# Two transformer blocks on one core: orders in the head loops and the cross attention, constants moved, heads gated in pairs, and the meta values as one product of two stacked parts

## What is computed

```
z = rms(h) @ w_in;  q, k, v, glu, g_att, g_conv = split(z)
a = softmax(q1 k1) - lam * softmax(q2 k2);  o = a @ v          # 8 heads, keys: 16 meta + 256
u = conv31(glu_a * sigmoid(glu_b));  y_conv = silu(layernorm(u)) @ w_conv_out
h = h + (sigmoid(g_att) * rms(o) * 0.8 + sigmoid(g_conv) * y_conv) @ w_out
h = h + (silu(gate) * val) @ w_down                            # gate, val: conv3(rms(h) @ w_up)
# second block
y_a = attention(rope(q), rope(k), v) @ w_br_attn               # 16 heads
S_t = diag(f_t) S_{t-1} + (1 - f_t) i_t^T;  o_t = S_t^T q_t    # 8 heads
h = h + (sigmoid(g_a) * y_a + sigmoid(g_b) * y_b) @ w_out
h = h + softmax((h wq) (mem wk)^T) (mem wv) @ wo               # 4 heads
h = h + (silu(gate) * val) @ w_ffn_out;  out = rms(h)
```

## Time and profile before

| | us |
|---|---|
| median of 3 runs | 1175.7 |
| lowest, highest | 1172.73, 1177.06 |
| the profiled execution | 1175.38 |
| its span, first to last instruction | 1173.8 |
| PE busy in the span | 1116.6 (95%) |
| DVE, ACT, POOL busy | 721.7, 600.1, 639.6 |
| mean granted clock of TensorE | 0.981 |

### The profile page before, as it was taken

One profiled execution on the slowest core, in us unless ns is written; L12 is line 12 of the kernel. 1 busy time (PEld: TensorE's weight loads), 2 busy tenths in 40 slices (PEclk: granted clock), 3 DMA queues, 4 the chain that ended last, 5 costly groups with the idle time before them and its releaser, 6 DMA issues.

```text
span 1173.8 us, 24755 instructions
## 1 busy us (share of the span) xinstructions
PE 1116.6 (95%) x8858; PEld 1078.5 (92%) x8858; DVE 721.7 (61%) x1435; ACT 600.1 (51%) x1124; POOL 639.6 (54%) x452
## 2 busy tenths in 40 slices
PE   6999999999889999999899999999999999999997
PEld 6999999998779999999889888998989989999996
DVE  5675766689656777625767584857766546444322
ACT  5654444455256656437555455555645455544332
POOL 5666767660355666643654535354466446656642
PEclk9999999999889999998899999999999999999998
DMA  8443444342343454543433233333444434555541
GB/s 326 145 152 139 168 138 157 143 149 72 144 180 131 165 195 167 202 148 138 162 112 133 100 144 142 143 107 143 180 146 178 144 108 180 185 180 206 182 144 36
DMA packets 26210, 179.43 MB, mean 153 GB/s; under 512 B 2849, under 2 KB 4129, under 8 KB 4769
## 3 DMA queue, kind: packets, MB, share of 16 engines
q1 hardware_dynamic: 25856, 178.28, 42.4%
q10 hardware_dynamic: 288, 0.27, 0.1%
HBM read 177.49 MB, written 1.05 MB: 152 GB/s over the span
## 4 chain that ended last, share of the span: by engine, by line
PE 65%; DVE 17%; issue 9%; POOL 4%; ACT 3%; DVEq 1%; DMA 0%; POOLq 0%; ACTq 0%
PE ps L573 43%; PE ps L855 10%; POOL parts L418 3%; DVE act L2064 2%; PE ps L639 2%; DVE parts L418 1%; ACT parts L1135 1%; PE ps L488 1%; DVE ps L2205 1%; DVE act L1832 1%; PE ps L670 1%; DVE branch L1973 1%; POOL sq L2335 1%; PE ps L897 1%; PE ps L613 1%
## 5 line engine op out<-in xcount | busy, mean ns | idle before, releaser
L418 POOL TENSOR_TENSOR parts<-ring,parts 128x1024 fp32r<-128x1024 f32 x208 | 511.9, 2472 | 434.1 <-ACT parts L1135 431.1
L573 PE MATMUL ps<-x_high,parts 128*128 128x256 f32 (+2 forms) x3088 | 419.1, 284 | 1.5 <-POOL parts L418 1.5
L573 PEld LDWEIGHTS ps<-x_high,parts 128*128 128x128 f32 x3088 | 387.7, 189 | 10.8 <-issue 5.6
L1135 ACT ACTIVATE parts<-ring 128x1024 fp32r<-128x1024 f32 x324 | 324.0, 1049 | 138.3 <-PE ps L855 69.3
L418 DVE TENSOR_TENSOR parts<-ring,parts 128x1024 fp32r<-128x1024 f32 x116 | 155.6, 1341 | 138.5 <-ACT parts L1135 138.5
L573 PE MATMUL ps<-x_low,parts 128*128 128x256 f32 (+2 forms) x1520 | 214.3, 283 | 0.0
L573 PEld LDWEIGHTS ps<-x_low,parts 128*128 128x128 f32 x1520 | 196.1, 189 | 0.0
L1759 DVE SCALAR_TENSOR_TENSOR ps<-glu,table_sb,ps 128x256 f32<-128x256 f32 x232 | 93.3, 480 | 0.6 <-DVE ps L1759 0.5
L855 PE MATMUL ps<-act_high,parts 128*128 128x256 f32 x704 | 87.8, 279 | 0.0
L855 PEld LDWEIGHTS ps<-act_high,parts 128*128 128x128 f32 x704 | 85.1, 188 | 0.0
L573 PE MATMUL ps<-parts,x_high 128*128 128x256 f32 x448 | 65.0, 295 | 3.4 <-DVE work L2121 3.4
(11 more groups left out here) (347 smaller groups left out, 1580.3 us busy)
## 6 DMA issues: line engine op xcount, KB each, us to landing
ring<-weights SPq DMA_DIRECT2D x166, 1024.0 KB, 4.8
res<-h_in SPq DMA_DIRECT2D x4, 272.0 KB, 3.8
act<-mem SPq DMA_DIRECT2D x1, 1024.0 KB, 14.6
out<-xT SPq DMA_DIRECT2D x4, 256.0 KB, 2.4
table_sb<-table SPq DMA_DIRECT2D x1, 969.5 KB, 9.0
table_sb<-table ACTq DMA_DIRECT2D x1, 132.5 KB, 3.5
work<-positions ACTq DMA_DIRECT2D x1, 128.0 KB, 5.4
```

What stands on the lines that cost most here:

```text
L418: eng.tensor_tensor(parts[:, LOW - HIGH + p, cols], ring[:, slot, cols], parts[:, p, cols].bitcast(F32), ALU.subtract)\
L573: mm = pe.matmul(out, left(k), right(k), start=step_ == 0 and k == 0, stop=step_ == 2 and k == KB - 1)
L1135: sc.activation(parts[:, p, cols], ring[:, slot, cols], ACT.Copy).then_inc(split_high, 1)
```

## The change

It has eight parts.

1. **Meta values.** A new tile `stacked` holds the high part of the 16 meta tokens in columns 0 to 15, the low part in columns 64 to 79, and zeros between. POOL fills it before the remainder of chunk 1. Tile 5 multiplies it by the high and by the low weights, 16 matmuls of 256 columns in place of 24. The two sets of 16 rows are added in the products behind, for which ACT writes the turned probabilities twice (`a1M`, `aMT`).
2. **First head loop.** DVE runs two of the taps before `combine1(2)`, and `conv_lead` behind it.
3. **Gating.** Heads 4 to 7 are gated two at a time, with mixing and remainders between.
4. **Constants.** The small constants (`constants2`) and their exponential (`bound_exps`) move into the down projection of the first block: on DVE behind the low half of chunk 3, ahead of `mirrored_constants`, on ACT behind the high parts of chunk 4.
5. **Entry of the second head loop.** The tanh and the product for the first query tile run before the logarithms and the cumulative sums; so they do for every next pass, at the end of the pass before. The last pass stands outside ACT's loop.
6. **Inside a pass.** `level(i, 0, 5)` runs before `rope(q_r)`. For head 1 `maxima2` runs before the low half of chunk 7, and the two `normalise2` before `low_values` and `gather1`. On ACT `turned2` runs before `decay(11)`.
7. **Branches.** `low_b(2)` runs before `gate_b(3)`.
8. **Cross attention.** `turn_x(h - 2)` runs before `scores_x(h - 1)`, and the products of `cross_out` that need only the finished heads are spread between the last turns and values.

```diff
@@ split_by_token @@
-                for start_token, at in ([(0, CW)] if extra else []) + [(first_token, 0)]:
-                    x = lambda part: lambda k: part[:, k, start_token:start_token + P]
...
+                if extra:
+                    pe.wait_ge(meta_stacked, 1)
+                    for part in (high, low):
+                        for k in range(KB):
+                            pe.matmul(ps[0:STACK, b, CW:2 * CW], stacked[:, k, :], w(part)(k), start=part is high and k == 0,
+                                      stop=part is low and k == KB - 1)
...
@@ gpsimd @@
+                    gp.tensor_copy(stacked[:, :, 0:META], x_high[:, :, 0:META])
+                    gp.tensor_copy(stacked[:, :, 64:STACK], x_low1[:, :, 0:META]).then_inc(meta_stacked, 1)
@@ pair1, DVE @@
+                conv_taps(i * 2, 0, 2)
+                combine1(2)
                 conv_lead(i * 2)
-                combine1(2)
-                conv_taps(i * 2, 0, 4)
+                conv_taps(i * 2, 2, 4)
@@ gating, DVE @@
+            mix(0)
+            mix(1)
+            low_mixed1(0)
+            ve.wait_ge(bank_read[7], 1 + 4 * 4 + 1 + 2)
+            root_heads(4, 2)
+            low_mixed1(1)
+            mix(2)
+            gate_heads(4, 2)
+            low_mixed1(2)
+            mix(3)
+            root_heads(6, 2)
+            low_mixed1(3)
+            mix(4)
+            gate_heads(6, 2)
+            low_mixed1(4)
@@ down1, DVE and ACT @@
-            down_low("down1", mirrored_constants)
+            down_low("down1", lambda: (constants2(), mirrored_constants()))
-            down_high("down1")
+            down_high("down1", bound_exps)
@@ before heads2, ACT @@
-            sc.wait_ge(cum_ready, 2)
+            tanh2(0, 0, tanh_q[:, 0, :], tanh_ready)
+            load_table(ACT.Ln)
+            for first, end in ((0, 2), (2, KB)):
+                sc.wait_ge(forget_ready, end)
...
+            sc.activation(small[:, 28:29], col("eps6"), ACT.Tanh)
@@ heads2, DVE @@
                 level(i, 0, 4)
+                level(i, 0, 5)
                 ve.wait_ge(rotated, n.next(rotated))
                 rope(q_r)
                 gather0()
-                level(i, 0, 5)
...
                 cross_level(i, 1)
+                maxima2()
                 low_v("heads2", i, 7)
-                low_values(i, 0)
-                maxima2()
-                gather1()
                 normalise2(0)
                 normalise2(1)
+                low_values(i, 0)
+                gather1()
@@ branches, DVE @@
+            low_b(2)
             gate_b(3)
-            low_b(2)
@@ cross attention, PE @@
+                if h >= 2:
+                    turn_x(h - 2)
                 if h >= 1:
                     scores_x(h - 1)
                 if h >= 2:
-                    turn_x(h - 2)
                     values_x(h - 2)
...
+            out_products(out_high, ox_high, range(4), begin=True)
             turn_x(3)
+            out_products(out_high, ox_low, range(4))
             values_x(3)
```

More of the change, by code:

```diff
@@ L309, in blocks_kernel @@
         a1M = carve(work, 4212, P)
+        stacked = rounded("stacked", [P, KB, STACK], "work", 1832)
         qM = carve(work, 4598, HEADS, LEAD)
@@ L1085, in _, with out_products @@
             values_x(2)
+            out_high, out_low = weight_parts("cross_out", 0)
+            out_banks = [STREAM.bank("cross_out", e) for e in range(2)]
+            def out_products(w, x, ks, begin=False, end=False):
+                for k in ks:
+                    for e in range(2):
+                        mm = pe.matmul(ps[:, out_banks[e], 0:SEQ], w[:, k * CW + e * P:k * CW + e * P + P], x[:, k, :],
+                                       start=begin and k == 0, stop=end and k == KB - 1)
+                        if end and k == KB - 1:
+                            mm.then_inc(tile_done, 1)
+            pe.wait_ge(split_high, STREAM.split("cross_out", 0, 0) * 2)
+            for e in range(2):
+                hold(pe, tile_read[out_banks[e]], STREAM.before("cross_out", 0, e))
+            out_products(out_high, ox_high, range(4), begin=True)
             turn_x(3)
+            out_products(out_high, ox_low, range(4))
             values_x(3)
-            last_products = split_late("cross_out", ox_high, ox_low, SEQ, None, 2)
+            out_products(out_high, ox_high, range(4, 6))
+            out_products(out_high, ox_low, range(4, 6))
+            wait_low("cross_out", 0, 0)
+            out_products(out_low, ox_high, range(6))
             hold(pe, bank_read[6], n.now(bank_read[6]))
-            last_products()
+            for w, x, end in ((out_high, ox_high, False), (out_low, ox_high, False), (out_high, ox_low, True)):
+                out_products(w, x, range(6, KB), end=end)
             for c in range(1, 4):
@@ L1418, in _ @@
             high_parts("heads2", 0, 1, STREAM.done("forget", 0, 7))
-            load_table(ACT.Ln)
-            sc.wait_ge(forget_ready, KB)
-            for first, end in ((0, 2), (2, KB)):
-                part = conv_f[:, first * SEQ:end * SEQ]
-                sc.activation(part, part, ACT.Ln).then_inc(log_ready, 1)
             def reuse(x):
@@ L1468, in hgrn_output, with tanh2, heads2 @@
                 sc.activation(oh[:, i * 2 + h, :], ps[:, 3, 0:SEQ], ACT.Copy).then_inc(bank_read[3], 1)
-            sc.wait_ge(cum_ready, 2)
-            with sc.Fori(0, 4) as i:
-                n.enter("heads2", i)
+            def tanh2(i, t, out, sem_):
+                sc.wait_ge(tile_done, STREAM.done("heads2", i, t))
+                sc.activation(out, ps[:, STREAM.bank("heads2", t), 0:SEQ], ACT.Tanh, scale=0.5).then_inc(sem_, 1)
+            tanh2(0, 0, tanh_q[:, 0, :], tanh_ready)
+            load_table(ACT.Ln)
+            for first, end in ((0, 2), (2, KB)):
+                sc.wait_ge(forget_ready, end)
+                part = conv_f[:, first * SEQ:end * SEQ]
+                sc.activation(part, part, ACT.Ln).then_inc(log_ready, 1)
+            sc.activation(small[:, 28:29], col("eps6"), ACT.Tanh)
+            def heads2(i):
                 def copy2(t, out, width=SEQ, **kw):
```

81 lines of the change are left out of this document (47 added, 34 removed).

## The result

The changed kernel takes 1161.3 us (median of four runs, 1156.9 to 1163.4) against 1175.6; the ratio is 0.988, 95% interval 0.986 to 0.990. The forecast was 1147 with a range from 1137 to 1160: the gain is 14.3 where 28 was expected. The profiled execution took 1163.4, its span is 1161.7 and its mean granted clock 0.979 (before: 1175.4, 1173.8, 0.981).

A forecast was written before the change was run, and what follows sets the result against it. TensorE bounds the kernel, busy 1116.6 of 1173.8 us, so time is its work plus its waits. Terms 6.4 + 5.8 + 2.7 - 6.7 + 5.4 + 12.0 + 1.4 + 1.2 = 28.2 took 1175.4 to 1147; range 1137 to 1160.

The forecast's parts named there:

- Start and first loop: Meta values and first head loop: 3.8 from fewer matmuls, 3.1 from combine1(2) waits, less 0.5 for POOL copies; gain 6.4 us.
- Gating: conv_out: pairs of heads make remainders ready in time, so mix_out1 starts at 307.3, not 313.1; gain 5.8 us.
- chunk behind it: Behind mix_out1's start: with the small constants gone, chunk 2's parts come just ahead of PE; gain 2.7 us.
- Down projection: Moved constants and a blocked copy make chunk 4's low half late: wait 4.5, slow stretch 2.2; loss 6.7 us.
- Entry: Second loop's start: early tanh removes the first query product's wait and slow stretch, 0.5 new wait; gain 5.4 us.
- The pass of the second loop: Level waits 9.4 go, 1.2 more gained, 2.0 lost, two slow stretches 3.4 go; gain 12.0 us, bounds 6 and 14.
- one hold-up of 1.5 a pass: Rival: in the second loop moved products meet another POOL instruction each pass, 6 less gain, 1153 us; chance 0.15.
- slow stretches standing elsewhere: Rival: the clock does not come back, as many slow stretches stand elsewhere, 8.7 us lost, 1156 us; chance 0.1.
- The rival that ended slower than before: Second loop: maxima2 ahead of chunk 7's low half waits for late scores, deciding from 8.5 us a pass; chance 0.03.
- The prediction's sign of being wrong: Second loop's passes staying over 61 us each, against 64 before and 60 of PE work.
- Branches: low_b(2) frees PE 2.8 sooner, but low_b(3) and chunk 1 are late; gain 1.4 us, bounds 0 and 3.
- cross attention: Waits for turned probabilities and a softmax shrink, but turn_x(2) follows late; gain 1.2 us, bounds 0 and 2.

The follow-up runs named there:

- levels_alone: Kernel before the change with one edit: level 5 of head 0 early, ahead of the query turning and gather0; 1164.0 us, ratio 0.989.
- tail_as_before: Changed kernel with the whole order behind the levels of head 1 in the second loop as before, level 5 still early; 1148.9 us, ratio 0.978.
- maxima_split: split_constants with head 1's masking sums ahead of chunk 7's low half, reductions behind it, value remainder behind gather2; 1138.6 us, ratio 0.970.
- constants_back: Changed kernel with the small constants and their exponential back ahead of the first sum of mix_out1; 1154.5 us, ratio 0.982.
- gather_first: Changed kernel with value remainder and gather1 back ahead of the normalisation, chunk 7's low half still behind the maxima; 1157.9 us, ratio 0.984.
- split_constants: tail_as_before with the constants spread over three chunks of the down projection; 1143.2 us, ratio 0.972.
- chunk_first: Changed kernel with chunk 7's low half ahead of the maxima again in head 1 of the second loop; 1153.1 us, ratio 0.981.

## Why the prediction failed, and where it held

**Start and first loop** (6.4): 5.9. The stacked product is 16 matmuls where 24 stood, and of three waits for `combine1(2)` none is left. The two POOL copies cost less than the 0.5 taken: the wait for chunk 1 grows from 0.5 to 1.4, but PE is there 0.7 sooner, and the product behind it starts at 24.86 instead of 24.60. Missed was one wait of 1.0 that is new in the first pass. It stands behind four DVE products that take 3.64 beside POOL, where the next four take 1.42.

```profile
24.86 2.27 PE L576 MATMUL ps<-x_high,parts 128*128 128x272 f32 x16 [1.40 <-POOL parts L421]
32.48 2.24 PE L604 MATMUL ps<-parts,stacked 128*80 128x256 f32 x16
45.24 0.28 PE L715 MATMUL ps<-table_sb,work 128*16 128x128 f32 x1 [1.01 <-DVE work L1760]
```

**Gating** (5.8) and the **chunk behind it** (2.7): 5.4 and 3.3, by the mechanism given; the kernel with the first alone is 4.5 faster. Against the earlier trace rows all of `conv_out` is one row, and `mix_out1` waits 0.64 for the mixing of tile 6, where 0.8 was forecast:

```profile
272.56 28.61 PE L491 MATMUL ps<-conv,ring 128*128 128x258 f32 x128
301.81 1.92 PE L647 MATMUL ps<-mixed_high,parts 128*128 128x258 f32 x14 [0.64 <-ACT mixed_high L1339]
```

**Down projection** (-6.7): -5.4. The wait is 3.9 (forecast 4.5), and the slow stretch behind it costs 1.4 (forecast 2.2: 32 matmuls in 5.29 instead of 3.93). DVE waits 4.36 for ACT's exponential, and one of the copies meets POOL as forecast:

```profile
482.89 0.93 DVE L1988 TENSOR_TENSOR small<-small 128x8 f32<-128x8 f32 x1 [4.36 <-ACT small L1375]
...
487.14 2.38 DVE L2065 COPY table_sb<-conv 128x64 f32<-128x64 f32 x1
...
492.59 5.29 PE L863 MATMUL ps<-act_high,parts 128*128 128x256 f32 x32 [3.92 <-DVE parts L421]
```

The same copy takes 0.20 on either side. The reductions between the copies keep their 0.28, but none of them stood beside a POOL product, so the other half of the port rule, that reductions never contend (the Trainium skill, SBUF — State Buffer, Who interferes with whom), isn't shown here.

**Entry** (5.4): 4.8 in the changed kernel, 5.9 alone (with the 1 of the clock named above), with a new wait of 0.44 (forecast 0.5). The drain of 1380 ns behind a table load, which the Trainium skill (ScalarE: Activation LUTs, What ACT_TABLE_LOAD costs) has and the prediction left out, shows at neither of the two loads of this place:

```profile
565.11 1.28 ACT L1175 ACT_TABLE_LOAD   x1
566.40 0.20 ACT L1175 ACTIVATE small<-table_sb 128x1 f32<-128x1 f32 x1
...
568.52 1.28 ACT L1509 ACT_TABLE_LOAD   x1
569.82 0.20 ACT L1509 ACTIVATE small<-table_sb 128x1 f32<-128x1 f32 x1
```

**The pass of the second loop** (12.0): -4.8. This is the term that failed. Its half on the level was right: 9.7 us of the loop by levels_alone. The failed step is what the term took for the new order behind the last level of head 1: "`maxima2` first takes a wait of 0.3 a pass at `turn2`. The wait that `maxima2` adds on DVE is covered: the scores are there." That was booked as a gain of 1.2 in four passes. The scores were there and the 0.3 is gone, but in its place PE waits 2.45 a pass for `gather2` at the values of head 1.

The walk that the prediction shows, with "`gather2` is then no earlier than before, and PE waits some 0.4 for it", is that of head 0, and there it was nearly right. POOL's half of chunk 5 does hold DVE up, though it meets a product behind the turning of the keys, and `gather2` still comes in time, without the wait of 0.4:

```profile
592.34 2.49 DVE L2115 TENSOR_TENSOR res<-work,res 128x128 f32<-128x128 f32 x1
592.22 2.46 POOL L421 TENSOR_TENSOR parts<-ring,parts 128x1024 fp32r<-128x1024 f32 x1
```

For head 1, whose order was changed, the prediction shows no such walk. There the low half of chunk 7 now comes behind POOL's half and takes 3.1 instead of 1.2. The prediction itself had the price of such a meeting (a copy of 2.42 for 0.21) and used it in the down projection and at the turning of the keys. Nor did it see that `gather1` had been what covered ACT's exponentials. Either miss alone is enough for a wait of about 2: with the low half put back PE waits 2.2 a pass, with `gather1` put back 1.74 and up to 0.30, with both put back 0.81 and 0.30, and as changed 2.45. Even the best of these is a wait of 1.1 where the prediction had 0.4 in the whole pass. With it the loop gains 10.5, so the 12.0 were somewhat high even without the new order.

The second part is the clock. Two slow stretches of 3.4 were to go; in their place came four, 24 us in all, which at half speed is up to 12 us of the loop. The rivals had each piece alone, one hold-up of 1.5 a pass (1153) and slow stretches standing elsewhere (1156). They were weighed as separate cases, but the wait that comes back can bring its slow stretch with it. The two together, 28.2 - 6 - 8.7 from 1175.4, are 1162, close to the result, and that is in part luck: 5.3 of the 8.7 were for the gating and the entry, whose slow stretches did go, while the loop's new ones cost more than its 3.4. The bounds of the term, 6 and 14, had no case with both. Added up, the bounds of all terms leave about 9 on the bad side and 40 on the good one, not 6 and 39.

The rival that ended slower than before named this very edit, the maxima ahead of the low half of chunk 7, but priced only late scores. They were not late. What it cost came from the other side, the low half itself. The prediction's sign of being wrong, passes that stay over 61, did come: the changed kernel's take 63.6, 64.9 and 64.9 from one pass's first mirrored values to the next, those of tail_as_before 60.7, and those of maxima_split 59.5 to 59.6, under the 60 that the prediction had as PE's work.

**Branches** (1.4) and **cross attention** (1.2): 1.2 and 1.6. `low_b(3)` is late by 1.41 (forecast 1.5), chunk 1 by 1.40 (forecast 1.7).

What stays open: why a wait of 2.45 has 0, 3.4 or 6.8 us at half speed behind it. The runs show that its length doesn't settle it (constants_back, and two groups of runs of one kernel), and that a wait under 2 can have one too (gather_first: 1.74, then 3.4 in each pass).

## What to carry to other kernels

When an instruction on VectorE is moved, walk its whole queue again with POOL's instructions beside it, up to the end of every part whose order changes, and price every product of two SBUF inputs that lands behind a POOL product at that product's remaining time more. A short instruction behind which an engine waits for another one's result is the place to put independent work, and taking such work away costs as much as a wait. Where a wait of TensorE may come back, price it with a slow stretch behind it as one case, and not the two apart.

## What the runs showed of the hardware

- Slow stretches of TensorE were 3.4 or 6.8 us long (but for the one at the end of each kernel), in the kernel before too: those of its gating and its entry ran from 298.7 and 578.6 for 6.8, and the earlier trace rows shows the part in which PE works. The changed kernel in eight runs took from 1156.0 to 1166.1, at mean clocks of 0.987 to 0.976. The four kernels whose longest wait in the loop is 0.9 or less had no slow stretch there in their profiles (levels_alone, tail_as_before, split_constants, maxima_split).
- Who pays when the two meet goes by the order of arrival: a low half that starts 0.9 ahead of POOL's takes 1.22 and POOL's 2.59; one that starts 0.3 behind takes 3.14 and POOL's 2.38.
- Instructions of DVE that read PSUM were not held up in the same stage: in chunk_first the two masking sums of the maxima take 0.76 and the four reductions 0.28 to 0.41 beside POOL's product of 673.23 to 675.71, the same as in the changed kernel, where POOL's starts with the last of them.
